# A triangular inverse on TensorE: the second product of each doubling level written to the other half of the partitions, in a bank of its own

## The reference, cut to what matters

```python
a_low = jnp.where(strict, jnp.einsum('nbhcd,nbhsd->nbhcs', kb, kc) * decay, 0.0)
tmat = a_low + jnp.eye(C, dtype=f32)
w = lax.linalg.triangular_solve(tmat, kb * jnp.exp(gc)[..., None], left_side=True, lower=True, unit_diagonal=True)
u = lax.linalg.triangular_solve(tmat, vc * bc[..., None], left_side=True, lower=True, unit_diagonal=True)
...
def step(s, inp):
    v_new = u_i - jnp.einsum('bhcd,bhde->bhce', w_i, s)
    ...
```

## Time and profile before

| | |
|---|---|
| median of 3 runs | 2056.06 us (2052.41 to 2056.16) |
| the profiled execution, its own time | 2060.62 us |
| its span | 2058.8 us |
| TensorE busy | 1944.4 us |
| VectorE, ScalarE, GpSimd busy | 724.5, 507.0, 362.7 us |
| scan of layer 0 and of layer 1, in the span | 395 to 664 us, 1481 to 1693 us |

### The profile page before, as it was taken

How to read it: one execution, slowest core, us unless ns; L and a number is a source line. 1 busy time by engine, 2 the same in 40 slices (tenths; PEclk the granted TensorE clock), 3 DMA queues, 4 the chain that set the end, 5 groups by cost and what they waited for, 6 DMA issues and landing times.

```text
span 2058.8 us, 41161 instructions
## 1 busy us (share of the span) xinstructions
PE 1944.4 (94%) x17601; PEld 1266.4 (62%) x17601; DVE 724.5 (35%) x1507; ACT 507.0 (25%) x1079; POOL 362.7 (18%) x411
## 2 busy tenths in 40 slices
PE   6999999899999998999999899999889999999998
PEld 4565567678888554555555445556688885455554
DVE  3154344344443334111121325334345442523223
ACT  4211533432222222010100131343332222210001
POOL 1512000333341002200010032100135330000000
PEclk7999999999999999999999999999899999999999
DMA  9410000344444215999999612100100002489996
GB/s 326 126 41 21 21 1 1 114 158 153 149 141 145 73 51 175 310 347 312 328 325 316 229 41 62 42 0 21 53 13 13 23 3 104 162 342 408 414 408 263
DMA packets 196888, 320.65 MB, mean 156 GB/s; under 512 B 10761, under 2 KB 163119, under 8 KB 189583
## 3 DMA queue, kind: packets, MB, share of 16 engines
q1 hardware_dynamic: 184928, 287.20, 39.6%
q0 software_dynamic: 6432, 20.00, 3.5%
q10 hardware_dynamic: 5390, 11.44, 1.6%
HBM read 305.45 MB, written 13.16 MB: 155 GB/s over the span
## 4 chain that ended last, share of the span: by engine, by line
PE 82%; DMA 5%; DVE 5%; ACT 4%; issue 2%; SPq 1%; POOL 1%; DVEq 0%; ACTq 0%; POOLq 0%
PE psum L564 16%; PE psum L962 7%; PE psum L1104 5%; PE psum L1056 5%; PE psum L1082 5%; PE psum L684 3%; PE psum L1167 3%; PE psum L893 3%; DMA ring<-in_moe_w_up 3%; PE psum L905 3%; PE psum L1063 2%; PE psum L908 2%; PE psum L729 2%; PE psum L704 2%; PE psum L501 2%
## 5 line engine op out<-in xcount | busy, mean ns | idle before, releaser
L564 PE MATMUL psum<-hT,ring 128*128 128x256 f32 (+2 forms) x976 | 336.8, 502 | 4.2 <-ACT hT L1481 3.8
L564 PEld LDWEIGHTS psum<-hT,ring 128*128 128x128 f32 (+1 forms) x976 | 184.0, 191 | 144.5 <-issue 126.8
L1056 PE MATMUL psum<-ring,arena 128*64 128x256 f32 x1024 | 126.4, 403 | 25.3 <-DMA ring<-in_moe_w_up 15.2
L962 PE MATMUL psum<-hT,ring 128*128 128x512 f32 (+1 forms) x384 | 139.4, 521 | 0.9 <-DVE xT L2261 0.9
L905 PE MATMUL psum<-ring,wbuf 64*64 64x64 f32 x1920 | 123.3, 226 | 3.7 <-DVE wbuf L2226 2.8
L908 PE MATMUL psum<-wbuf,ring 64*64 64x64 f32 x1920 | 121.1, 224 | 0.0
L2533 POOL TENSOR_TENSOR mlaw<-ring,lev 128x512 f32<-128x512 f32 x72 | 91.1, 1270 | 165.0 <-PE psum L893 162.6
L1056 PEld LDWEIGHTS psum<-ring,arena 128*64 128x64 f32 x1024 | 76.3, 145 | 68.8 <-issue 36.7
L2348 DVE TENSOR_TENSOR arena<-arena,psum 128x384 f32<-128x384 f32 (+1 forms) x32 | 15.6, 488 | 291.1 <-PE psum L1063 191.7
L962 PEld LDWEIGHTS psum<-hT,ring 128*128 128x128 f32 x384 | 72.7, 190 | 64.8 <-issue 61.5
L905 PEld LDWEIGHTS psum<-ring,wbuf 64*64 64x64 f32 x1920 | 103.8, 140 | 7.3 <-issue 5.3
(11 more groups left out here) (330 smaller groups left out, 3294.3 us busy)
## 6 DMA issues: line engine op xcount, KB each, us to landing
ring<-in_moe_w_gate SPq DMA_DIRECT2D x64, 1024.0 KB, 10.1
ring<-in_ada_w SPq DMA_DIRECT2D x48, 1024.0 KB, 5.2
ring<-in_moe_w_up SPq DMA_DIRECT2D x48, 1024.0 KB, 8.1
ring<-in_moe_w_down SPq DMA_DIRECT2D x32, 1024.0 KB, 11.2
ring<-in_w_in SPq DMA_DIRECT2D x20, 1024.0 KB, 5.9
big<-in_moe_w_down SPq DMA_DIRECT2D x16, 1024.0 KB, 14.5
ring<-in_w_out SPq DMA_DIRECT2D x8, 1024.0 KB, 5.1
xT<-in_moe_w_up SPq DMA_DIRECT2D x8, 1024.0 KB
```

The costliest lines, as they stand in the source:

```text
L564: m = pe.matmul(b[0:c1 - c0, 0:n], lhsT=w[:, k, c0:c1], rhs=hT[:, k, t0:t0 + n], start=k == 0, stop=k == KD - 1)
L962: m = pe.matmul(b[:, 0:x], lhsT=w[:, k, c:c + P], rhs=mixT[:, k, t0:t0 + x], start=k == OUT_REST[0], stop=k == OUT_GDN[-1])
L1056: m = pe.matmul(b[e * CAP_L:(e + 1) * CAP_L, 0:2 * P], lhsT=xs[:, k, e, 0:CAP_L], rhs=w[e][:, k, :], start=k == 0, stop=k == KD - 1)
```

## The change

The transposed inverse of a block is kept on the other partition half from the one on which the inverse lies. So the second product of a level is written to the other half (`across`), in a bank of its own, and the four products of a head lie in four 64x64 quarters of TensorE: (rows 0-63, output 0-63), (64-127, 64-127), (0-63, 64-127), (64-127, 0-63). To suit it:

- `t0` goes across; `z` takes both its operands from the other half and goes back;
- the masked matrices of levels 1 and on are needed on the other half: DVE writes a second, swapped copy `gAS` of the diagonal blocks (two more 64x256 operations for each kk piece), and POOL masks that one;
- a level claims two more banks (four in place of two), signals twice, and ACT copies 128x256 twice for each direction, the transposed one (`xb`) first;
- `z` waits only for the copy of `xb`, the next `x` for that of `x`; `z6`, `u6` and POOL's copies likewise.

```diff
+        gAS = at(dT[:, :, :].rearrange("p c t -> p (c t)"), 2 * SLOT_COLS, (2, GH, HALF))
...
+                across = [(rows_of[r], rows_of[1 - r]) for r in range(2)]
...
-                            for r in rows_of:
-                                m = pe.matmul(b[r, h * HALF:(h + 1) * HALF], lhsT=gML[0][r, d, h, :], rhs=eye[r, :],
+                            for r, o in across:
+                                m = pe.matmul(b[o, h * HALF:(h + 1) * HALF], lhsT=gML[0][r, d, h, :], rhs=eye[r, :],
                                               start=True, stop=True)
...
-                            evacuated(pe, ("x", l, j, d, n - 1) if n > 1 else ("t0", l, j, d))
+                            evacuated(pe, ("xb", l, j, d, n - 1) if n > 1 else ("t0", l, j, d))
                             for h in range(GH):
-                                for r in rows_of:
-                                    m = pe.matmul(b[r, h * HALF:(h + 1) * HALF], lhsT=gML[n % 2][r, d, h, :],
-                                                  rhs=x[r, d, 1, h, :], start=True, stop=True)
+                                for r, o in across:
+                                    m = pe.matmul(b[r, h * HALF:(h + 1) * HALF], lhsT=gML[n % 2][o, d, h, :],
+                                                  rhs=x[o, d, 1, h, :], start=True, stop=True)
...
-                            key = ("x", l, j, d, n)
+                            key, other = ("x", l, j, d, n), ("xb", l, j, d, n)
                             b = claim(key)
+                            b2 = claim(other)
+                            if n > 1:
+                                evacuated(pe, ("x", l, j, d, n - 1))
                             evacuated(pe, ("z", l, j, d, n))
                             for h in range(GH):
                                 for r in rows_of:
-                                    pe.matmul(b[r, h * HALF:(h + 1) * HALF], lhsT=gW[r, d, h, :],
-                                              rhs=x[r, d, 0, h, :], start=True, stop=True)
-                                for r in rows_of:
-                                    m = pe.matmul(b[r, (GH + h) * HALF:(GH + h + 1) * HALF], lhsT=x[r, d, 0, h, :],
-                                                  rhs=gW[r, d, h, :], start=True, stop=True)
+                                    m = pe.matmul(b[r, h * HALF:(h + 1) * HALF], lhsT=gW[r, d, h, :],
+                                                  rhs=x[r, d, 0, h, :], start=True, stop=True)
+                                for r, o in across:
+                                    m2 = pe.matmul(b2[o, h * HALF:(h + 1) * HALF], lhsT=x[r, d, 0, h, :],
+                                                   rhs=gW[r, d, h, :], start=True, stop=True)
                             done(m, key)
+                            done(m2, other)
...
-                            key = ("x", l, j, d, n)
-                            b = product_ready(act, key)
-                            read_out(act.copy(gXC[j % 2][:, d, :, :, :].rearrange("p x h c -> p (x h c)"), b), key)
+                            for w, name in ((1, "xb"), (0, "x")):
+                                key = (name, l, j, d, n)
+                                b = product_ready(act, key)[:, 0:GH * HALF]
+                                read_out(act.copy(gXC[j % 2][:, d, w, :, :].rearrange("p h c -> p (h c)"), b), key)
...
                             dve.tensor_tensor(gAC[c, d, :, :], b[c, :, c], gEB[d][c, :, c], ALU.mult)
+                            dve.tensor_tensor(gAS[rows_of[1 - r], d, :, :], b[c, :, c], gEB[d][c, :, c], ALU.mult)
                         c, r = rows_of[d], rows_of[1 - d]
-                        read_out(dve.tensor_tensor(gAO[j % 2][r, :, :], b[r, :, c], gEB[d][r, :, c], ALU.mult), key)
+                        read_out(dve.tensor_tensor(gAO[j % 2][c, :, :], b[r, :, c], gEB[d][r, :, c], ALU.mult), key)
...
-                    pool.tensor_tensor(gML[n % 2], gAC, lev[:, :, n, :].unsqueeze(2).to_broadcast([P, 2, GH, HALF]),
+                    pool.tensor_tensor(gML[n % 2], gAS if n else gAC, lev[:, :, n, :].unsqueeze(2).to_broadcast([P, 2, GH, HALF]),
                                        ALU.mult).then_inc(s["ml"], 1)
...
-                    link(pool.tensor_copy(gX[rows_of[0], :, :, rows_of[0]], gXC[j % 2][rows_of[0], :, 1, :, :]), l)
-                    pool.tensor_copy(gX[rows_of[1], :, :, rows_of[1]], gXC[j % 2][rows_of[1], :, 1, :, :]
+                    link(pool.tensor_copy(gX[rows_of[0], :, :, rows_of[0]], gXC[j % 2][rows_of[1], :, 1, :, :]), l)
+                    pool.tensor_copy(gX[rows_of[1], :, :, rows_of[1]], gXC[j % 2][rows_of[0], :, 1, :, :]
                                      ).then_inc(s["xd"], 1)
```

More of the change, by code:

```diff
@@ L914, in _ @@
                     for d in range(2):
-                        evacuated(pe, ("x", l, j, d, LEVELS - 2))
+                        evacuated(pe, ("xb", l, j, d, LEVELS - 2))
                     for h in range(GH):
                         for d in range(2):
-                            m = pe.matmul(b[rows_of[d], h * HALF:(h + 1) * HALF], lhsT=gAO[j % 2][rows_of[1 - d], h, :],
-                                          rhs=x[rows_of[1 - d], d, 1, h, :], start=True, stop=True)
+                            m = pe.matmul(b[rows_of[d], h * HALF:(h + 1) * HALF], lhsT=gAO[j % 2][rows_of[d], h, :],
+                                          rhs=x[rows_of[d], d, 1, h, :], start=True, stop=True)
                     done(m, key)
@@ L924, in _ @@
                     evacuated(pe, ("z6", l, j))
+                    for d in range(2):
+                        evacuated(pe, ("x", l, j, d, LEVELS - 2))
                     for h in range(GH):
@@ L2573, in _ @@
                     for d in range(2):
-                        evacuated(pool, ("x", l, j, d, LEVELS - 2))
+                        evacuated(pool, ("xb", l, j, d, LEVELS - 2))
                         if j:
```

## The result

| | before | changed |
|---|---|---|
| median of 4 runs each, us | 2055.38 (2052.41 to 2056.16) | 2030.9 (2024.42 to 2032.22) |
| the profiled execution, its own time | 2060.62 | 2024.42 |
| its span | 2058.8 | 2022.6 |

The ratio is 0.9886, 95% interval 0.9868 to 0.9905, that is 24 us faster between the medians (20 to 27 by the interval), where 30 was predicted. A second measurement of the same kernel gave 2026.31 us and 0.9859 [0.9838, 0.988], 29 us; the two together stand on both sides of the forecast of 2026.

A forecast was written before the change was run, and what follows sets the result against it. PE was taken to bound the kernel, though it also waits before level 4's `z`. Savings of 21 us in layer 0 and 16 in layer 1, less 7 for the clock, took 2056 to 2026 us; range 2014 to 2050.

The forecast's parts named there:

- Full overlap: Level `x` phases: four quarter products run side by side, a phase falls from 1.86 to 0.93 us, at most 56 us.
- Rival D: Quarters on the same rows don't overlap, a phase stays at 1.86 us, kernel slower at 2062 us; chance 0.12.
- Rival C: PE can't take in instructions fast enough: 25 ns each, a phase takes 1.6 us, kernel 2051 us; chance 0.11.
- The decay chain: Layer 0, chunks 1 to 4: ACT's copy and decay DMA set level 4's `z`; levels 2 and 3 save 0.70 each chunk.
- Layer 0: First layer's scan and start: 11.2, 2.8, 2.4 and 4.7 us saved by chunk and level, 21 in all before the clock.
- The starts: Scan starts: POOL's first mask waits for DVE's longer kk pieces, 0.5 us later in layer 0, 1.4 in layer 1.
- Layer 1, kk: Chunks 0 to 4: five DVE operations hold back `gW` of level 5; levels 4 and 5 save 1.1, not 1.9.
- 5.5 + 6.3 + 4.2 + 0.3: Layer 1 savings: levels 4 and 5 of chunks 0-4; levels 1-3 of chunks 1-4; chunk 5; chunk 0; sum 16 us.
- The last chunk's loop: Layer 1, chunk 5, levels 3 to 5: a level takes 2.53 us instead of 3.31, saving 0.78 each, 2.3 us.
- The clock: Longer holes before level 4's `z` bring half clock: four more times in layer 0, two in layer 1, 7 us given back.
- Rival B: Full overlap and the clock stays up in longer holes, or holes stay short: 2019 us, at best 2000; chance 0.07.
- Costed at nothing: POOL's masks and other-half reads, two more banks, second signal and wait, ACT's 120 extra copies except where counted: no time.

## Why the prediction was right

- **Full overlap, 0.93 us a phase: right.** 0.94 us. Rival D (same rows don't overlap) falls with the phases of 0.94 us, in the changed order and with the same rows next to each other. By the Trainium skill (page "TensorE: Matmul & The Clock Gate", Part 3, The mechanism), weight loads overlap only with another row group; here, with 64x64 tiles, four weight loads and four matmuls start in 0.058 us on two row halves, each load 0.14 us long and each matmul over 0.2, so the measurement decides against it. Rival C falls too: one record every 14.5 ns (0.058 / 4). That is below the 25 ns of Part 1 of that page of the Trainium skill. But what C feared, that instructions come too slowly, did happen in another form, at the four stops.
- **The decay chain, 0.70 us saved a chunk in levels 2 to 4: right in kind, sized somewhat low.** From the first record of `x` of level 2 to `z` of level 4 chunks 1 to 4 take 9.70, 9.44, 10.49 and 9.55 us and took 11.14, 10.52, 10.87 and 10.53: 1.44, 1.08, 0.38 and 0.98, 0.97 on the mean. The holes before `z` of level 4 in layer 0 grew less than told: 1.88, 2.94 and 1.99 us in chunks 2 to 4 (1.12, 1.47, 1.12 before), where 2.4 to 3.0 was told, and 0.69 in chunk 1, whose `x` phase stopped. In layer 1 they are 2.4 to 3.0, as told. In all PE stood idle for 26.6 us before `z` and not 30 and more. In chunk 3 DVE waits longer for the DMA (before 1.10):

```profile
542.84 0.69 DVE L2161 TENSOR_TENSOR arena<-arena,small 128x512 f32<-128x512 f32 x1 [1.85 <-DMA arena<-decay_rows]
...
546.22 0.59 PE L895 MATMUL psum<-ring,mlaw 64*64 64x64 f32 x13 [2.94 <-ACT ring L1766]
```

- **Layer 0: 15.9 predicted for the scan (21, without the 0.5 of the start, less 5.6 for the clock), 13.6 measured, 16.0 when measured again.** Chunks 3 and 4 from `t0` to `t0` (46.92 for chunk 4, 47.26 for chunk 3 before) save 2.9 and 3.5 us, where 3 x 0.93 + 0.70 = 3.5 was told; chunk 2 saves 0.6, with an `x` phase at half clock (1.68 us at 501.83). Chunk 0 saves 1.4 and not 2.9 (2.4 and the 0.5 of the start): its `x` phase of level 3 runs at half clock behind a hole of 2.10 us. What I didn't have: the 4.8 us of stops for instructions, in chunks 1 and 5. And the banks, costed at nothing, aren't quite: in level 1 of five chunks the phase takes 1.12 us, because the second direction starts 0.18 us late. That it waits for its bank, which held the adaLN product that ACT has just read out (L1463, 528.12 to 528.29; L910 starts at 528.38), is the reading of the timeline alone. 0.9 us in all.
- **The starts, 0.5 and 1.4: right** (+0.6, +1.4). Without the second copy they are gone, but POOL's longer first inverse takes their place.
- **Layer 1, kk: the mechanism right, the term mis-sized.** Five operations now stand ahead of `gW`:

```profile
1514.60 0.42 DVE L2174 TENSOR_TENSOR ring<-psum,arena 64x256 f32<-64x256 f32 x1 [2.96 <-PE psum L814]
...
1516.25 0.42 DVE L2177 TENSOR_TENSOR ring<-psum,arena 64x256 f32<-64x256 f32 x1
1516.70 0.75 DVE L2236 TENSOR_TENSOR wbuf<-lev,psum 128x256 f32<-128x256 f32 x2
1517.27 0.27 PE L910 MATMUL psum<-ring,wbuf 64*64 64x64 f32 x2 [0.54 <-DVE wbuf L2236]
```

  They delay `x` of level 5 by 0.6 us (2.78 us behind its `z`, before 2.17), where I had taken levels 4 and 5 together at 1.1 saved in place of 1.9. The scan saved 16.8 us (18.1 when measured again); the terms give 5.5 + 6.3 + 4.2 + 0.3, plus the 1.4 of the start, less 1.4 for the clock: 16.3.
- **The last chunk's loop, 2.53 us: right, with some luck.** From `x` of level 4 (1650.23) to `x` of level 5 (1652.81) it is 2.58 us, before 3.31. But the parts named in the prediction add up to 2.65 us (1.20 + 0.14 + 0.47 + 0.26 + 0.42 + 0.16), a slip of 0.12 for each of three levels, which the measured loop makes half good.
- **The clock, 7 us given back: right in kind, on the low side.** Time at half clock in the two scans went from 3.4 and 17.1 us to 17.1 and 24.5 (10.2 and 17.0 when measured again). Filling the holes of layer 1 gives 2 to 4 us of its scan (193.4 and 194.7 to 191.3 and 190.4), where I had given that layer's clock 1.4. Rival B falls: the holes grew and the clock fell more often.
- **Costed at nothing:** more banks, signals and copies cost nothing in the kernel without the crossing; with it, the 0.18 us above. POOL's read from the other half: 363.4 us busy, before 362.7.

The stops and the banks take 5.7 us of layer 0 for which the sum had no term. That the total fits all the same is in part luck: other terms, the decay chain among them, gave more than told.

Of the 56 us that the shorter phases could give at most, 28 stay. The rest went into a chain that begins with ACT and a DMA and ends with ACT, into ACT's work in chunk 0, into DVE's longer kk pieces, into the clock behind longer holes, and into stops for instructions.

## What to carry to other kernels

Small matmuls in different quarters of TensorE ran side by side here when they were issued close together; write the order so that the quarters alternate record by record, as TensorE made up only part of a bad order (1.35 us, between 1.86 and 0.94). Before counting such a gain, follow what the next phase waits for: here half of it was lost to holes that opened up elsewhere and to the clock behind them. A filler matmul pays only where its bank is free at once and the hole is as long as the filler. And an edit that makes one engine's work shorter by splitting another's needs a look at the first wait behind it: POOL's 1.3 us more cost all that DVE's shorter start gave.

## What the runs showed of the hardware that I had not expected

- Products of 64x64 tiles on four quarters sustain one start every 14.5 ns over a phase of 64 records.
- Matmuls may start out of program order across quarters: with the products grouped, a phase took 1.35 us, between 1.86 and 0.94.
- TensorE stops for 0.3 to 1.4 us in a dense phase without a wait that the profile shows, 2.2 to 2.7 us behind the start of a 16 KB packet of the instruction queue. The stops of one layer stand a whole number of 256 records apart, and with 192 records put ahead they stand 192 places earlier.
- A DVE operation of 128x512 took 1.53 us in place of 0.69 while POOL worked on its own 128x512 one for 0.98 us of it, and 1.11 or 1.27 us with 0.56 or 0.73 us of overlap. No run removed POOL's operation alone.

What stays open: whether fewer banks claimed in level 1 would save the 0.18 us (not tried), what decides at which of the packets TensorE stops, and why the clock falls behind some holes of 1.9 to 3 us and not behind others in one and the same kernel: in the changed kernel it fell behind 1.88 us in chunk 2 of layer 0 and not behind 2.94 us in chunk 3.
